# One of four channel tiles of a depthwise convolution moves from VectorE to GpSimd

## The reference, cut to what matters

```
def conformer_conv_group(u, dw_w, dw_b, norm_g, norm_b):
    a, g = jnp.split(u, 2, axis=-1)
    h = a * jax.nn.sigmoid(g)
    h = jnp.pad(h, ((0, 0), (CONV_TAPS - 1, 0), (0, 0)))          # 31 taps, causal
    h = lax.conv_general_dilated(h, dw_w[:, None, :], window_strides=(1,), padding='VALID',
        dimension_numbers=('NWC', 'WIO', 'NWC'), feature_group_count=CONV_WIDTH) + dw_b
    h = layer_norm(h, norm_g, norm_b)
    return jax.nn.silu(h)
```

## Time and profile before

| what | us |
|---|---|
| median of 3 runs (3385.13 to 3387.68) | 3385.7 |
| the profiled execution's own time | 3385.13 |
| its span in the profile | 3382.6 |
| PE busy | 2896.7 (86% of the span) |
| DVE busy | 1170.3 (35%) |
| ACT busy | 751.2 (22%) |
| POOL busy | 241.1 (7%) |

### The profile page before, as it was taken

One profiled execution on the slowest core, in us unless ns is written; L12 is line 12 of the kernel. 1 busy time (PEld: TensorE's weight loads), 2 busy tenths in 40 slices (PEclk: granted clock), 3 DMA queues, 4 the chain that ended last, 5 costly groups with the idle time before them and its releaser, 6 DMA issues.

```text
span 3382.6 us, 31088 instructions
## 1 busy us (share of the span) xinstructions
PE 2896.7 (86%) x11890; PEld 1825.1 (54%) x11890; DVE 1170.3 (35%) x1663; ACT 751.2 (22%) x1169; POOL 241.1 (7%) x156
## 2 busy tenths in 40 slices
PE   7978888899989798788999959978888758777778
PEld 3324566688854235565888834648788444222223
DVE  0176234433330392544333334364444340000001
ACT  2133232322221242332212131141111022000001
POOL 0120000000000300000000006012332010000000
PEclk9989999999999899999999989889989869999999
DMA  4123211224230132211333231000000026999990
GB/s 143 50 75 120 80 50 57 68 81 113 84 113 22 50 136 88 75 50 50 87 94 100 81 109 44 32 25 1 1 1 1 0 87 275 410 409 410 409 381 25
DMA packets 256104, 379.57 MB, mean 112 GB/s; under 512 B 9153, under 2 KB 170078, under 8 KB 255838
## 3 DMA queue, kind: packets, MB, share of 16 engines
q1 hardware_dynamic: 255966, 377.72, 31.3%
HBM read 375.59 MB, written 2.10 MB: 112 GB/s over the span
## 4 chain that ended last, share of the span: by engine, by line
PE 66%; DMA 13%; DVE 12%; ACT 4%; issue 3%; POOL 1%; SPq 0%; DVEq 0%; ACTq 0%; POOLq 0%; PEldq 0%
PE banks L790 29%; PE banks L766 11%; PE banks L1093 9%; DMA ring<-in_w_up 8%; PE banks L1210 7%; DMA arena<-in_w_down 4%; DVE arena L2080 4%; PE banks L1362 2%; PE banks L776 1%; PE banks L782 1%; PE banks L1025 1%; PE banks L1340 1%; DVE stat L2061 1%; PE banks L1111 1%; DVE arena L2261 1%
## 5 line engine op out<-in xcount | busy, mean ns | idle before, releaser
L1549 ACT ACTIVATE w_hi<-ring 128x2048 fp32r<-128x2048 f32 (+1 forms) x100 | 174.4, 1746 | 544.2 <-PE banks L790 544.2
L790 PE MATMUL banks<-ffn_x_hi,w_hi 128*128 128x512 f32 x704 | 277.7, 394 | 16.7 <-DVE ffn_x_lo L1999 16.6
L790 PE MATMUL banks<-ffn_x_lo,w_hi 128*128 128x512 f32 x704 | 275.6, 391 | 0.0
L790 PE MATMUL banks<-ffn_x_hi,w_lo 128*128 128x512 f32 x704 | 275.4, 391 | 0.0
L1985 DVE TENSOR_TENSOR w_lo<-ring,w_hi 128x2048 fp32r<-128x2048 f32 (+1 forms) x100 | 207.5, 2077 | 78.8 <-ACT w_hi L1549 77.4
L1362 PE MATMUL banks<-ring,std 128*64 128x512 f32 x640 | 153.6, 603 | 46.3 <-DMA ring<-in_w_up 26.5
L766 PE MATMUL banks<-xT,ring 128*128 128x512 f32 (+1 forms) x416 | 183.5, 604 | 1.2 <-ACT taps L1453 1.2
L2080 DVE SCALAR_TENSOR_TENSOR arena<-arena,taps 128x512 f32<-128x512 f32 x240 | 163.3, 743 | 0.0
L790 PEld LDWEIGHTS banks<-ffn_x_hi,w_hi 128*128 128x128 f32 x704 | 132.9, 189 | 51.5 <-issue 17.9
L2449 DVE TENSOR_TENSOR gates<-gates,banks 128x512 f32<-128x512 f32 x16 | 11.0, 688 | 423.9 <-PE banks L1362 423.9
L1093 PE MATMUL banks<-zT,ring 128*128 128x512 f32 x320 | 144.7, 610 | 7.7 <-issue 6.9
(11 more groups left out here) (363 smaller groups left out, 4493.6 us busy)
## 6 DMA issues: line engine op xcount, KB each, us to landing
ring<-in_w_up SPq DMA_DIRECT2D x48, 1024.0 KB, 18.4
arena<-in_w_down SPq DMA_DIRECT2D x48, 1024.0 KB, 18.4
ring<-in_ffn_w_in SPq DMA_DIRECT2D x88, 512.0 KB, 4.5
ring<-in_w_gate SPq DMA_DIRECT2D x32, 1024.0 KB, 18.0
ring<-in_w_mod SPq DMA_DIRECT2D x24, 1024.0 KB, 7.2
ring<-in_xa_w_kv SPq DMA_DIRECT2D x16, 1024.0 KB, 6.2
zT<-in_w_gate SPq DMA_DIRECT2D x16, 1024.0 KB, 18.5
zT<-in_w_up SPq DMA_DIRECT2D x16, 1024.0 KB, 18.4
```

The costliest lines, as they stand in the source:

```text
L790: mm = pe.matmul(bank[:, :], weights(wp, k), rhs(rp, k), start=(k == 0 and wp == rp), stop=(k == n - 1 and wp == 1))
L1549: nc.scalar.activation(w_split[n % 2][0][:, 0:m], raw[n % 2][:, 0:m], ACT.Copy).then_inc(f_hi.sem, 1)
```

## The change

DVE keeps three tiles (`DT = CT - 1 = 3`). The fourth tile is computed by POOL, behind its part of the query rotation. POOL has no operation here that multiplies and adds at once, so each tap is two TENSOR_TENSOR: a product with the tap's weights, broadcast along the tokens, into one of the two halves of `squares`, and an addition to the running sum. For k = 0 the product goes straight to the sum, and the bias is added. This makes 62 instructions of 128x512 in each layer. A new semaphore `conv_pool` counts them. PE waits for its last count before the mean of the fourth tile, where it waited for DVE before. The buffer `mixT` and those that follow it move by 8 words (32 bytes), because the rounding of its start to 16 words is taken out, and the arena is 8 words shorter.

```diff
-ARENA = 26752
+ARENA = 26744
-        MIX = -(-(24 * S + KT * MEM + CT * (TAPS - 1 + S)) // 16) * 16
+        MIX = 24 * S + KT * MEM + CT * (TAPS - 1 + S)
-        conv = signal("conv", CT * TAPS)
+        DT = CT - 1
+        conv = signal("conv", DT * TAPS)
+        conv_p = signal("conv_pool", 2 * TAPS)
@@ PE
                 for t in range(CT):
-                    pe.wait_ge(conv.sem, conv.at(l, CT * (TAPS - 1) + t + 1))
+                    if t < DT:
+                        pe.wait_ge(conv.sem, conv.at(l, DT * (TAPS - 1) + t + 1))
+                    else:
+                        pe.wait_ge(conv_p.sem, conv_p.at(l, 2 * TAPS))
@@ POOL, behind the rotation of the queries
+                sums = mixT[:, CT + DT, :]
+                for k in range(TAPS):
+                    x, c = hpad[:, DT, k:k + S], taps[:, k * CT + DT:k * CT + DT + 1]
+                    c = c.broadcast_to([P, S])
+                    if k == 0:
+                        pool.wait_ge(qrot.sem, qrot.at(l, HEADS))
+                        nc.gpsimd.tensor_tensor(sums, x, c, ALU.mult).then_inc(conv_p.sem, 1)
+                        term = par[:, P_DWB + DT:P_DWB + DT + 1].broadcast_to([P, S])
+                    else:
+                        term = squares[:, k % 2, :]
+                        nc.gpsimd.tensor_tensor(term, x, c, ALU.mult).then_inc(conv_p.sem, 1)
+                    pool.wait_ge(conv_p.sem, conv_p.at(l, 2 * k + 1))
+                    nc.gpsimd.tensor_tensor(sums, sums, term, ALU.add).then_inc(conv_p.sem, 1)
@@ DVE
                 def tap(k):
-                    for t in range(CT):
+                    for t in range(DT):
...
-                            dve.wait_ge(conv.sem, conv.at(l, CT * (k - 1) + t + 1))
+                            dve.wait_ge(conv.sem, conv.at(l, DT * (k - 1) + t + 1))
```

## The result

The changed kernel takes 3446.8 us (median of 4 runs, 3444.46 to 3448.61), the kernel before took 3385.4 on the same chip (3381.96 to 3387.68). The ratio is 1.0182, with a 95% interval of 1.0165 to 1.02: 61.4 us slower. 3439 was forecast. The profiled execution took 3448.0 us, its span 3446.2.

A forecast was written before the change was run, and what follows sets the result against it. DVE's taps were taken to bound the attention loop, PE a close second. Per layer 29 - 0.5 (first tap) - 4.5 + 3 = +27 us, two layers +54: 3385.1 + 54 = 3439 us, range 3418 to 3464.

The forecast's parts named there:

- Turns: Attention loop: while POOL has work, each DVE tap costs a turn of tap plus POOL operation, 1.62 us (1.55 to 1.68).
- Rival 3: Attention loop: whole DVE and POOL instructions exclude each other, turn 2.01 us, +50 us a layer, 3485 us; chance 0.06.
- rival 4: Attention loop: POOL gets turns only between steps, gain and loss nearly cancel, about 3385 us; chance 0.02.
- Heads while POOL works: Attention loop: 12 turns plus 1.2 us make 20.6 us a head instead of 14.5; +29 us over 4.8 heads.
- After POOL's work: Rest of the attention loop: about 11 steps with three taps give back 7.5 us, less 3 for PE: -4.5.
- the sign set down: Forecast wrong if taps stay at 743 ns or the last chain before the loop's end runs through PE.
- PE's clock: Attention loop: PE waits at the scores and may drop to half clock; +3 us, bounds nothing and +13.
- Rival 2: Attention loop: half clock makes PE need 21.3 us a head, slower than DVE; +36 us a layer, 3457 us; chance 0.15.
- The wait at the mean: Before the fourth tile's mean: PE's new wait for POOL is covered by some 100 us and costs nothing.
- The upper bound of 36 us a layer: Loop's sum with turns of 1.68 us, 14 operations in a head and 8 us by the clock: 3457 us.
- the shift: mixT and following buffers moved by 32 bytes: within 1 us either way, taken as 0.
- Rival 1: Attention loop: DVE's taps don't wait for POOL, PE becomes the bound, 3363 us, faster; chance 0.05.

The follow-up runs named there:

- e_no_fourth: Against e_aligned: POOL's convolution replaced by one fill of zeros, the fourth tile left out of the computation; 3368.1 us, ratio 0.9941 to the kernel before.
- e_pool_late: Against e_aligned: POOL's 62 operations wait until DVE has done the loop's last tap; 3386.7 us against 3385.0 for the kernel before, ratio 1.0.
- e_pool_writes: Against e_aligned: POOL's convolution replaced by 62 fills of 128x1024, each behind a two-column product, fourth tile not computed; 3366.3 us, ratio 0.9946 to the kernel before.
- e_shift_only: Against the kernel before: only the start of mixT not rounded up, moving it by 32 bytes, convolution all on DVE; 3403.7 us, ratio 1.0051.
- e_aligned: The changed kernel without its shift: mixT's start rounded up to 16 words again, arena at its old size; 3428.2 us against 3387.4 before, ratio 1.0122.
- e_dve_late: Against the kernel before: the fourth tile's 31 taps moved behind the attention loop on DVE, no POOL convolution; 3367.5 us against 3387.4, ratio 0.994.

## Why the prediction was right, and where it was off

- **Turns.** Forecast 1.62 us (1.55 to 1.68), measured 1.56: POOL's 62 operations take 95.3 us (194.46 to 289.73), 1.54 each. e_no_fourth, e_pool_late and e_pool_writes show the cause: POOL's work beside the taps, and of that work what reads SBUF. The tap group's mean was forecast as 1.3 us, with six in ten taps at 1.6 to 1.8. It is 1.17, and half of the 180 taps last 0.84 us or less: the first tap of a step mostly doesn't wait. The Trainium skill (SBUF — State Buffer, section Who interferes with whom) says that a VectorE instruction with two SBUF inputs contends with a GpSimd instruction that reads SBUF and not with one that only writes it; the fills of e_pool_writes agree, 949 ns beside taps of 742. The Trainium skill (SBUF — State Buffer, section Summary: rules for kernel authors) adds that the second one to issue fully blocks until the first finishes. This does not hold to the letter: a product and a tap would need 1.04 + 0.74 = 1.78 us, a sum and a tap 2.01, and the turn is 1.56. Rival 3 (+50 a layer) is out, and so is rival 4, by which the taps would hardly have lost.
- **Heads while POOL works.** Forecast 20.6 us. Measured 21.3 and 21.1 where there is a head output, and 18.9 in the first two heads, from first tap to first tap (196.4, 215.3, 234.2), where there is none: the one operation more belongs to the output's copy and should have been left out there. POOL ends at 289.7 us (forecast 294), and the loss is 25.9 us at output 3, where 29 - 0.5 was forecast.
- **After POOL's work.** Forecast -4.5, measured -5.3 (25.9 to 20.6), and the bound is PE, as taken. By the sign set down (wrong if the last chain before the loop's end runs through PE) this would have spoken against the forecast; the sign was ill put, since PE can be the last link behind POOL's work whoever made the loss.
- **PE's clock.** Forecast +3; measured nothing that shows: from output 5 to 8 the distance to the kernel before stays at 20.6 to 21.1 us. The clock does fall while POOL works (0.84 on average from 215 us on), but PE then waits at the scores for 27.0 us in all, and these waits take it up. At the end of the loop it is as before: 4.49 us where the earlier trace rows have 4.53. Rival 2 (+36 a layer) is out.
- **The wait at the mean** doesn't arise, as said; e_pool_late shows its price where the cover is gone.
- **The product** takes 1.04 us alone (1.1 was used), less than the sum's 1.27.
- **Slips in the working.** The upper bound of 36 us a layer does not follow from its terms: with 14 operations in a head, 62 last 4.4 heads of +6.9, and the layer comes to about +33 (3452 us). And the trace before has the pair of both engines more than once: from 2091 us on the short convolution also runs beside POOL's L1871 of 1472 columns, and one of its instructions lasts 3.93 us there.
- **The loop's sum** is thus +20.9 for the first layer and +23 for the second, where +27 was forecast. In the first, 2.6 were too much for the heads, 3 for the clock, and 0.8 more were given back.
- **The failed term is the shift**: "within 1 us either way; nothing in the rows depends on it. I take 0." It costs 16.3 us by itself (e_shift_only), and without it the change costs 40.8 instead of 61.4. It moves ffn_x and xq_hi; the matmuls on ffn_x became some 7 ns longer each, and they alone make 13.8 us. The nearness of the forecast is in part luck: two errors stood against each other. The loops were 10 to 13 us too dear (54, against 43.7 by the spans of the profiles and 40.8 by the medians of e_aligned), and the shift 16 too cheap.
- **Rival 1** gave 3363 us for taps that don't wait for POOL. That kernel exists without POOL: 3368 (e_no_fourth) and 3367 us (e_dve_late). The sum for PE's pace was sound within 5 us, and only its condition false.

## What to carry to other kernels

Before work goes from DVE to POOL, look at what both read. Here the taps on DVE and POOL's operations, which all read SBUF, took turns, and POOL lengthened DVE's work instead of sharing it. Look instead for a stretch in which the loaded engine is idle and the consumer is late: here moving one tile's taps behind the loop on the same engine gave 20 us and moving two tiles' gave 23, where moving one to the other engine cost 41 (61 with the shift). A tap in one operation instead of two was not tried on POOL. And an edit that moves buffers is an edit of its own, to be timed by itself.

## What was not expected of the hardware

- The time of a 128x512 matmul with a 128x128 weight in these groups changes with where the buffers lie in SBUF. On ffn_x the medians are 389 ns in the old place, 396 ns 32 bytes lower, and 393 ns 128 bytes higher. 64 bytes higher, the three groups have means of 399, 394 and 390 ns, in the old place 394, 391 and 391. On ffn_hidden it is 389 ns throughout. On xq_lo, which does not move itself, the median goes from 389 to 393 and 397 ns. Small as it is, the effect of the 32 bytes makes 0.5% of the kernel's time.
- A POOL operation that reads two columns lasts 0.35 us longer beside a tap (0.55 instead of 0.20), and a fill of 1024 columns loses nothing.
- With nothing beside it, the product with an operand that is broadcast takes 1041 ns on POOL, the sum of two full operands 1267 (medians of e_pool_late).
- A cast on DVE with a single input from SBUF also waits for POOL: 1.25 us beside its operations, 0.42 without.
